# Attention and scan stage of a hybrid encoder layer: the order of VectorE's work on the next tile's decay steps, and of one norm

## The reference

```python
p = jax.nn.softmax(sc.astype(jnp.float32) * scale, axis=-1)     # per head, 128 queries against 512 or 1024 keys
o = einsum('bhqk,bkhd->bqhd', p, v);  return _rmsnorm(o, attn_norm_w)

cs = jnp.cumsum(dt * a.reshape(g, r), axis=2)                   # per chunk of 128 tokens and head
seg = cs[:, :, :, None] - cs[:, :, None, :]
decay_in = jnp.exp(jnp.where(lower, seg, -jnp.inf))             # 128 x 128 per head and direction
m = cb[..., None] * decay_in * dt[:, :, None]
y_diag = jnp.einsum('bcqsgr,bcsgrp->bcqgrp', m, x)
```

## Time and profile before

| | us |
|---|---|
| median of 3 runs | 2827.03 (2824.35 to 2827.82) |
| the profiled execution's own time | 2827.1 |
| its span, first to last instruction | 2825.3 |
| attention stage within it | 334 to 834 |
| one short tile (tile 2) | 29.7 (398.2 to 427.9) |
| one long tile (tile 7) | 42.8 (614.9 to 657.7) |

### The profile page before, as it was taken

One profiled execution on the slowest core, in us unless ns is written; L12 is line 12 of the kernel. 1 busy time (PEld: TensorE's weight loads), 2 busy tenths in 40 slices (PEclk: granted clock), 3 DMA queues, 4 the chain that ended last, 5 costly groups with the idle time before them and its releaser, 6 DMA issues.

```text
span 2825.3 us, 51607 instructions
## 1 busy us (share of the span) xinstructions
PE 2720.3 (96%) x18382; PEld 2399.0 (85%) x18382; DVE 2139.6 (76%) x4073; ACT 1530.6 (54%) x2894; POOL 228.0 (8%) x222
## 2 busy tenths in 40 slices
PE   7999888999999969999999999999999999999996
PEld 6989555666677859999999999999999999999996
DVE  4565887767765687877878878878878788788786
ACT  4443546454453345555555565555556555555565
POOL 0000431212200000000000000000000000000000
PEclk9999999999999989999999999999999999999998
DMA  7211312122146447767767768778677677687685
GB/s 282 66 64 58 129 39 78 55 108 84 75 151 216 149 162 241 254 230 245 252 220 249 258 223 259 230 240 269 220 251 245 228 249 253 221 260 243 225 276 205
DMA packets 359946, 548.24 MB, mean 194 GB/s; under 512 B 14816, under 2 KB 287968, under 8 KB 359840
## 3 DMA queue, kind: packets, MB, share of 16 engines
q1 hardware_dynamic: 352448, 520.88, 53.6%
q0 software_dynamic: 7392, 25.96, 4.3%
HBM read 494.30 MB, written 52.49 MB: 194 GB/s over the span
## 4 chain that ended last, share of the span: by engine, by line
PE 59%; DVE 3%; ACT 1%; issue 0%; DMA 0%; DVEq 0%; POOLq 0%; SPq 0%; POOL 0%; ACTq 0%
PE banks L3334 26%; PE banks L3347 16%; PE banks L3335 12%; PE banks L3307 4%; DVE weights_low L3096 1%; PE banks L3290 1%; ACT weights_high L2995 0%; DVE h_or_keys_or_sums L3220 0%; DMA weighted<-residual 0%; DVE hidden_parts L3235 0%; ACT h_or_keys_or_sums L3048 0%; DVE hidden L3230 0%; DVE rows L3178 0%; DVE keys_or_w_out L3178 0%; DVE weighted L3178 0%
## 5 line engine op out<-in xcount | busy, mean ns | idle before, releaser
L3334 PE MATMUL banks<-rowsT_parts,weights_high 128*128 128x384 f32 x4096 | 1236.0, 356 | 3.4 <-DVE hidden_parts L3235 2.1
L3335 PE MATMUL banks<-rowsT_parts,weights_low 128*128 128x192 f32 x4096 | 1025.7, 250 | 0.0
L3335 PEld LDWEIGHTS banks<-rowsT_parts,weights_low 128*128 128x128 f32 x4096 | 781.1, 191 | 1.2
L3334 PEld LDWEIGHTS banks<-rowsT_parts,weights_high 128*128 128x128 f32 x4096 | 769.2, 188 | 7.7 <-issue 4.3
L3096 DVE TENSOR_TENSOR weights_low<-keys_or_w_out,weights_high 128x1024 fp32r<-128x1024 f32 x512 | 603.8, 1217 | 1.4 <-ACT weights_high L2995 1.4
L2995 ACT ACTIVATE weights_high<-keys_or_w_out 128x1024 fp32r<-128x1024 f32 x512 | 523.9, 1049 | 21.9 <-PEq L2371 21.9
L3021 ACT ACTIVATE h_or_keys_or_sums<-banks 128x192 f32<-128x192 f32 x512 | 165.8, 324 | 438.3 <-PE banks L3307 305.3
L3220 DVE TENSOR_TENSOR h_or_keys_or_sums<-banks,h_or_keys_or_sums 128x192 f32<-128x192 f32 x512 | 181.6, 355 | 291.5 <-ACT h_or_keys_or_sums L3021 290.1
L3347 PE MATMUL banks<-weights_high,hidden_parts 128*128 128x512 f32 x1512 | 397.5, 391 | 1.6 <-DVE hidden_parts L3235 1.6
L3347 PEld LDWEIGHTS banks<-weights_high,hidden_parts 128*128 128x128 f32 x1512 | 278.9, 188 | 57.3 <-issue 2.0
L3096 DVE TENSOR_TENSOR weights_low<-slab_down,weights_high 128x1024 fp32r<-128x1024 f32 x256 | 311.5, 1217 | 0.0
(11 more groups left out here) (406 smaller groups left out, 3752.6 us busy)
## 6 DMA issues: line engine op xcount, KB each, us to landing
keys_or_w_out<-w_gate SPq DMA_DIRECT2D x128, 1024.0 KB, 5.1
keys_or_w_out<-w_up SPq DMA_DIRECT2D x128, 1024.0 KB, 6.9
slab_down<-w_down SPq DMA_DIRECT2D x128, 1024.0 KB
arena_attend<-w_ada SPq DMA_DIRECT2D x8, 2048.0 KB, 7.9
attention<-ssd_tiles SPq DMA_DIRECT2D x12, 992.0 KB, 8.8
ssd_tiles<-arena_inputs SPq DMA_DIRECT2D x24, 256.0 KB, 2.0
mixed<-attention SPq DMA_DIRECT2D x12, 512.0 KB, 2.8
residual<-arena_output SPq DMA_DIRECT2D x12, 512.0 KB, 2.6
```

Of the source, the lines that this page charges most:

```text
L3334: nc.tensor.matmul(out[:, 0:2 * CT], w_hi[:, u, block], x[:, k, :], start=k == 0, stop=False)
L3335: mm = nc.tensor.matmul(out[:, 0:CT], w_lo[:, u, block], x[:, k, 0:CT], start=False, stop=k == KD - 1)
```

## The change

On VectorE, `steps` and the high part's `terms` for the next tile are called in slot 1, behind the copy of the transposed probabilities (before: slots 2 and 3), and the low part's `terms` in slot 2 (before: slot 7). `norm_o` in slot 4 is called behind `tops` instead of ahead of it. Nothing is added or removed, and the programs of the other four engines stay as they are.

```diff
@@ on_dve, body
                 if h in (1, 2):
                     weights(g, h - 1)
-                if before and h == 4:
-                    norm_o(g - 1, 1 - j)
                 if h + 1 < NH:
                     tops(g, h + 1)
                 elif more:
                     tops(g + 1, 0)
+                if before and h == 4:
+                    norm_o(g - 1, 1 - j)
                 if not r and not more and h == 7:
...
                 if follows and h < 6:
                     front(h + 1, g + 1, place, 1 - j)
+                if follows and h == 1:
+                    steps(g + 1, 1 - j)
+                    terms(g + 1, 1 - j, 0)
                 if follows and h == 2:
-                    steps(g + 1, 1 - j)
-                if follows and h == 3:
-                    terms(g + 1, 1 - j, 0)
-                if follows and h == 7:
                     terms(g + 1, 1 - j, 1)
                 if h == 4:
                     add_off(g)
```

## The result

The changed kernel took 2836.01 us in the median of 7 runs (2829.99 to 2838.58), the kernel before 2827.03 in 7 runs beside them. The ratio is 1.0030, with a 95% interval of 1.0021 to 1.0039. That is 9 us slower, inside the range given (2822 to 2839), but twice the 4.2 that were summed and past the 5.7 us called measurable. The seven times lie in two groups: 2829.99 and 2830.17, with a mean granted clock of 0.991, and five from 2835.93 up, with 0.987 to 0.988. The profiled execution is the first of them: a span of 2828.2 us against 2825.3, so it holds only 2.9 of the 9.

A forecast was written before the change was run, and what follows sets the result against it. Short tiles were taken as bound by TensorE and VectorE in turn, VectorE's SBUF products colliding with GpSimd's. Short tiles +4.2 us, long tiles 0: 2827.1 + 4.2 = 2831.3, or 2831.2 on the median's scale; range 2822 to 2839.

The forecast's parts named there:

- Steps 1 to 7: Short tile 2: VectorE and GpSimd alternate, 1.84 us stall in slot 3, slot 5's 1.23 gap closed, tile +0.91 us.
- step 6: Short tile 2: GpSimd's L2260 waits for the moved norm; `add_off` ends at 420.90 instead of 419.99, +0.91 us.
- Long tiles: Seven tiles, 4 to 10: head 3's exponentials start later but stay covered by 0.3 to 0.4 us; 0 us.
- TensorE's clock: Half-clock stretches behind gaps, some 3 us each: one fewer 2828.3, chance 0.15; one more 2834.1, chance 0.10.
- likeliest case: Whole kernel: no measurable change, within 0.2% (5.7 us), on the slow side; chance 0.62.
- signs of being wrong: L1924 keeping its 0.68, long tiles changing length, or clock stretches of 0.5 showing elsewhere in the windows view.
- late record: Next tile's record lands 3 us late, VectorE waits in slot 1 of long tiles: +8 us, 2839, chance 0.05.
- doubled port cost: Taken into the range's upper end, 2839; port costing more per tile than summed was given 0.08.
- clock rival: Behind TensorE's gaps, one more half-clock stretch, some 3 us: 2834.1, chance 0.10; one fewer: 2828.3, chance 0.15.
- No blocking: Spreads with repeated operands use the port less, slot 5's gap nearly goes: -4 us, 2823, chance 0.12.
- GpSimd twice in a row: GpSimd keeps the port for both spreads, `weights` ends 1.8 us later again: +22 us, 2849, chance 0.08.

The follow-up runs named there:

- e2: Changed kernel with GpSimd's two spreads over four of eight heads, half the backward decay left out: 2827.05 us, ratio 1.0000.
- e6: Changed kernel with GpSimd's two spreads waiting for VectorE's low spread instead of for the split: 2829.26 us, ratio 1.0004.
- e3: Kernel before with split and both spreads moved as in the change, norm left ahead of the row maximum: 2834.92 us, ratio 1.0027.
- e8: Kernel before with only the norm moved behind the row maximum: 2825.59 us, ratio 0.9999.
- e1: Changed kernel once more, unaltered, with more runs: 2834.36 us, ratio 1.0023.
- e5: Changed kernel with nine unused 128x128 products on TensorE filling slot 3's gap in short tiles: 2828.49 us, ratio 1.0008.
- e4: Kernel before with split and high spread between slot 2's row maximum and copy, norm behind row maximum, low spread in slot 7: 2823.07 us, ratio 0.9989.

## Why the prediction was right or wrong

**Steps 1 to 7, right nearly to the tenth.** Set back by the tile's offset of 3.40: head 3's bias 411.27 (predicted 411.29), its transposes 412.29 (412.31), VectorE's low spread ends at 413.47 (413.5), head 5's bias 417.81 (417.73), L2259 418.53 (418.46), `add_off` ends at 420.97 (420.90). The stall is 1.66 instead of 1.84, the gap of slot 5 is closed, L300 is at 0.28, slot 7 won nothing, the tile grew by 0.98 (0.91). e2 and e6 show the port as the cause: less of it, or at another time, and the gap of slot 3 shrinks or goes. e3 and e8 bear out that the norm buys nothing in step 6.

**Long tiles, step mis-sized: 0.9 us instead of 0.** "There are 0.3 to 0.4 us to spare" was right for the exponentials, but the copy queued behind the bias on VectorE had none: it used to start at 632.39, and the bias now ends at 632.56. The other part, 0.30 of idle time ahead of a later copy, goes with the spreads in slots 1 and 2: tile 7 is 43.17 to 43.29 long in e1, e2, e3, e5 and e6, and 42.83 to 42.84 in e4 and e8. Its cause stays open.

**TensorE's clock, the term that failed.** The prediction had it as one stretch more or fewer, 3 us, with a chance of 0.10 for one more, and its likeliest case as no measurable change. In the three profiled executions of kernels with the new gap unfilled (after, e1, e3) the clock fell to half right behind the gap of slot 3 in 6 of 12 short tiles; in the kernel before nothing of the kind lies between slot 3 and slot 5. One such stretch costs 1.6 us (32.26 against 30.70 in e1). An estimate from these: 4 x 0.5 x 1.6 = 3.2; with 3.0 for tiles 1 to 3, 1.5 for tile 0 (31.55 in e1, where it ran at full clock, against 30.01 before) and 0.9 for the long tiles that makes 8.6, against 9.0 and, in e1, 7.8 measured.

The 5.4 us without the clock (3.0, 1.5 and 0.9) are read from tiles at a like clock; 4.5 of them stand against the 4.2 summed for short tiles, and the 0.9 of the long ones is the port's only in part. The 3.2 are an estimate from above, since they count what slot 3 draws and nothing that falls away elsewhere. In the whole stage, with one of double length counted as two, the profiled execution of before had four stretches, that of after three, e1's six and e3's five. The mean granted clock is 0.9885 over the 27 runs of after, e1 and e3 that the ratios use and 0.9890 over those of before beside e1; each stretch takes off 0.0006 (1.7 of 2827 us), so that is about one stretch more and not two. Yet stretches don't all cost the same: ahead of the stage before's execution had three and after's one, and only 0.5 us was won by it. So the clock's share, something like 1 to 3 us, is argued and not shown, and whether it makes up the whole rest of the loss stays open.

e5 bears on it: with the gap filled and the port as it was, 4 to 6 us came back. Its profiled execution had two stretches in short tiles, both behind slot 7; e1 and e3 had five each, two in slot 3 and three behind slot 7. But its mean granted clock, 0.9909, is above even that of the kernel before beside it, 0.9888, so the extra products spared stretches that the kernel before has too. e5 shows that idle time of TensorE in these tiles draws half clock; it doesn't give the price of the new gap alone.

So the side was right, and so was the mechanism of the sum, and the likeliest case, no measurable change, was wrong. Two of the signs of being wrong that the prediction named came true: long tiles changed length, and stretches of half clock stood elsewhere. That the median still lies within 2822 to 2839 is partly luck: the part of the range above 2834 was there for a late record and a doubled port cost, and neither came. The step at fault is the clock rival's "One more: 2834.1, chance 0.10": the gap of 1.84 was entered in the sum by its length alone, and in its place half clock followed the gap of 1.66 in 6 of 12 short tiles, at 1.6 us each.

**The rivals.** No blocking is out (2.38 and 1.80). GpSimd twice in a row is out (its second spread went in behind `weights`). The record was in time: in long tile 7 the cast (L1894) follows its copy without a wait.

## What to carry to other kernels

Before moving a VectorE product of two SBUF operands, write down what GpSimd has ready at that moment and which instructions VectorE has queued behind: if those read PSUM, as in e4, the collision costs VectorE nothing; if the next is another such product, as `weights` was here, it waits out a whole GpSimd instruction (1.7 us). Moving work away from a gap is worth only as much as the place it goes to: the gap of 1.2 us was closed and one of 1.7 opened elsewhere. On TensorE a new gap cost its length and, in 6 of 12 cases here, 1.6 us of half clock behind it. In a tile held by one chain, look for the one instruction on it that could run an earlier slot (`add_off`, ready since slot 3): alone it gave 8 us, of which the lengths of the tiles explain some 4.5, where the best place found for the spreads gave 3.5.

## What the hardware showed that I had not expected

Gaps of much the same length are followed by half clock in one place and not in another. In slot 3, 1.66 us were followed by it in 6 of 12 cases. The 0.81 of e2 in the same place was in none of 4. In the three executions with 1.66 (after, e1, e3) the 1.14 to 1.32 ahead of slot 6's values were in none of 12, while slot 7, where two gaps (0.44 to 1.31, then 0.78 to 1.36) lie close together, was in 7 of 12. Where the gap ahead of slot 6's values had grown to 1.91 it was followed by half clock in 2 of 3 tiles of e8 and in none of 3 of e6. So neither length nor place alone decides, and what does is not shown. And two executions of one kernel, with all these gaps but one alike to 0.01 us, differed by 5.5 us (2829.99 and 2835.46): three stretches more in the stage make 4.7 of it, and one more ahead of the stage 0.7.
